# One-hot rows in steps of eight tokens, two coefficient blocks at a time, and one up product moved behind the last block

## The chip, the core and the metric

The kernel runs on one core of a Trainium2 chip. Its engines work side by side and meet through semaphores: TensorE multiplies matrices (PE in the profile; PEld is its weight load), VectorE (DVE), ScalarE (ACT) and GpSimd (POOL) do elementwise work, SyncE (SP) issues most DMA transfers. The metric is the device time of one execution in microseconds (us); lower is better.

## The reference

Two transformer blocks run over 256 tokens of width 1024. The first has two layers, each with a mixer and then a product-key mixture of experts ("peer"), which is where this change lies:

```python
q = (t @ w_q).reshape(n_tok, PEER_HEADS, 2, PEER_DKEY // 2)
sc = jnp.einsum('thpd,hpnd->thpn', q, sub_keys)
s1, i1 = lax.top_k(sc[:, :, 0], 16);  s2, i2 = lax.top_k(sc[:, :, 1], 16)
...                       # the best 16 of the 256 sums per head: eidx = i1 * 128 + i2
gate = jax.nn.softmax(top_s, axis=-1)
hid = jax.nn.gelu(jnp.einsum('td,thkd->thk', tc, u[ec]), approximate=False)
out = jnp.einsum('thk,thkd->td', gc * hid, v[ec])
```

There are 128 x 128 = 16384 experts, 8 heads and 16 choices per head, so 128 picks for each token. The second block (attention of two kinds and two feed-forward layers) isn't touched.

## The kernel before

The kernel computes the experts densely. It multiplies all tokens with all rows of `u` (the "up product": 128 chunks of 128 experts), takes the GELU, multiplies with a dense matrix of coefficients (the gate where a token picked that expert, zero elsewhere) and multiplies the result with `v` (the "down product"). Each f32 product is made of three: a weight tile in `ring` is split into `ring_hi` by ScalarE (`split_hi`, line 538) and `ring_lo` by VectorE (`split_lo`, line 544, which waits for `split_hi`), and TensorE multiplies `hi*hi`, `lo*hi` and `hi*lo` (lines 550 to 552). The ring has 4 slots of 512 KB; SyncE reloads a slot once `split_lo` has read it.

**The stage of the change** is segment `upcoef`, which runs once in each of the two layers. In it TensorE does 24 up products (8 steps of three matmuls each, so 192 steps, numbered q) and between them builds the coefficients, four tokens (one "block") at a time. The coefficients of a token are a product of one-hot matrices: `hot_second` (one row per pick, a one at the second key) as weights, and `hot_gated` (a one at the first key, times the gate, as a high and a low fp16 part) as the moving side. So a block is 4 x 2 = 8 matmuls of 128x128 in fp16 (line 910), after every third step; there are 64 blocks.

Who does what in the stage, for block c:

- VectorE (`one_hots`): `hot_first` (line 1999), `hot_second` (2000), then `hot_gated` from `hot_first` and the gates (2008, or 2004 where b = 0, for the low part alone). Before c % 8 = 2, 5 and 7 it does one `split_lo`.
- ScalarE (`gate_rows`, line 1376): the high part for the blocks with b = 0, in four instructions; it waits for `hot_first` of that block. It also copies each finished block out of PSUM in two instructions (`store_coef`, lines 1367 and 1368), takes the GELU of each finished up product (`gelu_beside`, 1352), does `split_hi`, and after every fourth block issues a DMA that spills half of the coefficients to DRAM (`spill`, 1382).
- TensorE (`coefficients`): waits for the PSUM bank (block c - 4 stored), `hots_ready` and, where b = 0, `act_gated`. The blocks of four are taken in the order 1, 0, 2, 3 (`ORDER`).

The order on each engine is written out by hand: for TensorE in the loop over q, for VectorE in the loop over c, for ScalarE in a loop over p, of which each turn ("pair") holds eight blocks and three up products. `split_hi` works two slots ahead of the up product in hand (`AHEAD` = 2): in turn p it makes slots 3p + 2, 3p + 3 and 3p + 4, while VectorE makes 3p + 1, 3p + 2 and 3p + 3. Behind the stage stand eight down products (line 896). The first of them needs `weigh(0)` on VectorE (lines 2029 to 2035), which needs the last block stored (`last_coef`) and, before the change, all 24 GELUs.

Of the kernel before, what the change touches and what calls it, by code (L numbers as in the profile page):

```python
# [24 lines left out]
P = 128  # L25
# [113 lines left out]
STEP_TOKENS = 4 * BLOCK  # L139
ORDER = [1, 0, 2, 3]  # L140
# [127 lines left out]
def build(nc, a):  # L268
    with ExitStack() as ctx:
# [20 lines left out]
        desk = sb("desk", [P, 3 * 2 * (P + 4 * HALF)])  # L290
        normed = desk[:, 0:K * TA].rearrange("p (k t) -> p k t", k=K)
        product = sb("product", [P, 2, S])
# [3 lines left out]
        rows = desk[:, :].bitcast(F16).rearrange("p (b n) -> p b n", b=3)  # L296
        last = product[:, :, :].rearrange("p b t -> p (b t)").bitcast(F16)
        hot_second = [x.rearrange("p (a e t) -> p a e t", a=2, t=2) for x in [rows[:, b, 0:P * BLOCK] for b in range(3)] + [rstd[:, 0:2 * P].bitcast(F16)]]
        hot_gated = [x.rearrange("p (x a e t) -> p x a e t", x=2, a=2, t=2) for x in [rows[:, b, P * BLOCK:3 * P * BLOCK] for b in range(3)] + [last]]
        hot_first = sb("hot_first", [P, 3, 2, NKEYS, 2], F16)  # L300
# [11 lines left out]
        gates16 = picks[:, 2:4, :].rearrange("p x s -> p (x s)").rearrange("p (k x t) -> p k x t", x=2, t=BLOCK)  # L312
# [83 lines left out]
        hidden = arena[:, 0:HELD * S].rearrange("p (h t) -> p h t", t=S)  # L396
        coef = arena[:, HELD * S:].rearrange("p (g t f) -> p g t f", t=S, f=BLOCK)
# [23 lines left out]
        val2raw = hot_first.rearrange("p b a e t -> p (b a e t)").bitcast(F32)[:, 0:2 * TA].rearrange("p (b t) -> p b t", b=2)  # L421
# [256 lines left out]
        def _(pe):  # L678
# [170 lines left out]
            def peer(l):  # L849
# [34 lines left out]
                def down(n, e, i=0, slots=4):  # L884
# [5 lines left out]
                    for t in range(NT):  # L890
                        by_hi, by_lo = [weighed[:, e % 4, x, t * P:(t + 1) * P] for x in range(2)]
# [8 lines left out]
                def coefficients(w, count):  # L900

                    b = count % 4

                    wait_bank(pe, w)
                    pe.wait_ge(hots_ready, count + 1)
                    if b == 0:
                        pe.wait_ge(act_gated, count // 4 + 1)
                    for t in range(BLOCK):
                        for x in range(2):
                            mm = pe.matmul(work[:, w % 4, t * P:(t + 1) * P], hot_second[b][:, t // 2, :, t % 2], hot_gated[b][:, x, t // 2, :, t % 2], start=(x == 0), stop=(x == 1))  # L910
                    mm.then_inc(bank_done[w % 4], 1)

                built = l * S // BLOCK
# [220 lines left out]
            def warm():  # L1134
                zeros = hot_first.rearrange("p b a e t -> p (b a e t)")
# [20 lines left out]
        def _(act):  # L1156
# [144 lines left out]
            def peer(l):  # L1301
# [48 lines left out]
                def gelu_beside(u):  # L1350
                    act.wait_ge(beside_done, l * BESIDE + u + 1)
                    act.activation(hidden[:, SEGMENTS[1][2] + u, :], acc[:, u % 4, 0:S], ACT.Gelu).then_inc(beside_free, 1)
# [17 lines left out]
                def gate_rows(j):  # L1370
                    act.wait_ge(gates_ready, l + 1)
                    act.wait_ge(hots_used, l * (S // BLOCK) + 4 * j + 1)
                    if j:
                        act.wait_ge(*done(W0[f"expert{l}.1"] + 4 * (j - 1) + ORDER.index(0)))
                    for t in range(BLOCK):
                        ins = act.activation(hot_gated[0][:, 0, t // 2, :, t % 2], hot_first[:, 0, t // 2, :, t % 2], ACT.Copy, scale=act_gates[:, j, t:t + 1])
# [8 lines left out]
                for x, (kind, e, h, steps) in enumerate(SEGMENTS):  # L1385
# [263 lines left out]
        def _(dve):  # L1649
# [318 lines left out]
            def peer(l):  # L1968
# [7 lines left out]
                by_block = lambda v: v.rearrange("p (k t) -> p k t", t=BLOCK)  # L1976
# [9 lines left out]
                def one_hots(count, tok, w):  # L1986

                    if w is not None:
                        dve.wait_ge(*done(w))
                    of = lambda x: picks[:, x, tok:tok + BLOCK]  # L1990
                    b, first = count % 4, hot_first[:, (0, 1, 2, 1)[count % 4], :, :, :]
                    if b == 0 and count:
                        dve.wait_ge(act_gated, count // 4)
                    if b and count > 4:
                        dve.wait_ge(hots_ready, count - 1)
# [429 lines left out]
```

## Time and profile before

| | us |
|---|---|
| median of 3 runs | 2471.43 (2470.43 to 2473.3) |
| the profiled execution | 2470.42 |
| its span in the trace | 2468.6 |
| TensorE busy | 2433.4 (99%) |
| VectorE busy | 1891.4 (77%) |
| ScalarE busy | 1256.3 (51%) |
| the stage of the change, each of two | about 106 |

The profile gives the busy time of each engine, the instructions by line with what ended the idle time before them, the waits by who waited for whom, and a timeline. "x8" in a timeline row means eight instructions merged; their start is that of the first. The mean of a short instruction is longer than the distance at which such instructions follow each other, since they are pipelined: the distance between two starts is what counts.

### The profile page before, as it was taken

To read this page: it belongs to the slowest core of one execution; us is meant where nothing else is said; L and a number is where in the kernel's file an instruction comes from. 1 tells how busy PE (TensorE), PEld (TensorE's weight loads), DVE (VectorE), ACT (ScalarE), POOL (GpSimd) and SP (SyncE) were. 2 spreads that over 40 slices of the span, in tenths; PEclk is the share of its full clock that TensorE was granted. 3 is DMA by queue.
4 is the path that set the end of the run, shared out by engine and by line. 5 is a ranking of instruction groups with operands and counts; after the bars stand their busy time and mean duration, and the time that the engine had idled before them with its cause. 6 is when DMAs were issued, how large, how long until landed. Compare 5 with 4: busy or idle time off the path is not lost.

```text
span 2468.6 us, 48181 instructions
## 1 busy us (share of the span) xinstructions
PE 2433.4 (99%) x17669; PEld 2253.8 (91%) x17669; DVE 1891.4 (77%) x3674; ACT 1256.3 (51%) x2092; POOL 132.4 (5%) x115
## 2 busy tenths in 40 slices
PE   9999999999999999999999999999999999999999
PEld 8999998999999888999988999999889999899999
DVE  6789997666666788889996666666887767887774
ACT  6755884444444434455874444444335445656343
POOL 0042000000000000052000000000000001100000
PEclk9999999999999999999999999999999999999999
DMA  7445677666665555546677666655554555634555
GB/s 241 143 158 184 191 204 249 207 214 213 210 200 188 188 187 171 189 146 201 188 219 236 213 210 207 213 196 188 187 187 144 174 183 182 142 103 156 182 182 165
DMA packets 191991, 465.16 MB, mean 188 GB/s; under 512 B 81530, under 2 KB 83706, under 8 KB 190944
## 3 DMA queue, kind: packets, MB, share of 16 engines
q1 hardware_dynamic: 118592, 419.47, 52.5%
q0 software_dynamic: 6624, 24.28, 3.3%
q10 hardware_dynamic: 66624, 19.40, 3.2%
q8 instruction: 94, 1.54, 0.3%
q14 instruction: 57, 0.47, 0.1%
HBM read 442.50 MB, written 20.59 MB: 188 GB/s over the span
## 4 chain that ended last, share of the span: by engine, by line
PE 49%; DVE 2%; ACT 1%; issue 0%; DMA 0%; DVEq 0%; ACTq 0%
PE acc L896 14%; PE work L550 9%; PE work L552 9%; PE work L551 9%; PE acc L550 2%; PE acc L551 1%; PE acc L552 1%; PE work L910 1%; PE work L1126 1%; DVE ring_lo L544 1%; PE work L1112 0%; PE work L1099 0%; DMA ring<-in_u 0%; ACT ring_hi L538 0%; PE work L1100 0%
## 5 line engine op out<-in xcount | busy, mean ns | idle before, releaser
L544 DVE TENSOR_TENSOR ring_lo<-ring,ring_hi 128x1024 fp32r<-128x1024 f32 (+1 forms) x757 | 918.8, 1217 | 421.0 <-ACT ring_hi L538 419.3
L538 ACT ACTIVATE ring_hi<-ring 128x1024 fp32r<-128x1024 f32 (+1 forms) x797 | 832.3, 1051 | 440.6 <-PE acc L896 359.8
L550 PE MATMUL work<-normed_hi,ring_hi 128*128 128x256 f32 (+1 forms) x2544 | 722.3, 284 | 10.2 <-DVE ring_lo L544 5.9
L551 PE MATMUL work<-normed_lo,ring_hi 128*128 128x256 f32 (+1 forms) x2544 | 713.3, 280 | 0.0
L552 PE MATMUL work<-normed_hi,ring_lo 128*128 128x256 f32 (+1 forms) x2544 | 713.3, 280 | 0.0
L896 PE MATMUL acc<-ring_hi,weighed 128*128 128x512 f32 x2048 | 587.3, 396 | 3.0 <-DVE weighed L2033 3.0
L550 PEld LDWEIGHTS work<-normed_hi,ring_hi 128*128 128x128 f32 x2544 | 478.7, 188 | 23.2 <-DVE ring_lo L544 7.1
L551 PEld LDWEIGHTS work<-normed_lo,ring_hi 128*128 128x128 f32 x2544 | 478.1, 188 | 8.3
L552 PEld LDWEIGHTS work<-normed_hi,ring_lo 128*128 128x128 f32 x2544 | 478.0, 188 | 0.0
L896 PEld LDWEIGHTS acc<-ring_hi,weighed 128*128 128x128 f32 x2048 | 372.2, 188 | 82.6 <-issue 3.2
L550 PE MATMUL work<-arena_parts,ring_hi 128*128 128x256 f32 (+1 forms) x1184 | 336.0, 284 | 2.8 <-DVE arena L2292 2.1
L552 PE MATMUL work<-arena_parts,ring_lo 128*128 128x256 f32 (+1 forms) x1184 | 332.4, 281 | 0.0
L551 PE MATMUL work<-arena_parts,ring_hi 128*128 128x256 f32 (+1 forms) x1184 | 332.4, 281 | 0.0
L896 PE MATMUL acc<-ring_lo,weighed 128*128 128x512 f32 x1024 | 321.4, 395 | 0.0
L1348 ACT ACTIVATE arena<-work 128x256 f32 (+1 forms) x192 | 73.8, 384 | 338.4 <-PE work L552 338.3
L896 PEld LDWEIGHTS acc<-ring_lo,weighed 128*128 128x128 f32 x1024 | 192.3, 188 | 46.4
L550 PEld LDWEIGHTS work<-arena_parts,ring_hi 128*128 128x128 f32 x1184 | 222.7, 188 | 4.6 <-DVE arena L2292 2.3
L551 PEld LDWEIGHTS work<-arena_parts,ring_hi 128*128 128x128 f32 x1184 | 222.8, 188 | 0.1
L552 PEld LDWEIGHTS work<-arena_parts,ring_lo 128*128 128x128 f32 x1184 | 222.6, 188 | 0.0
L2040 DVE TENSOR_TENSOR product<-arena 128x256 f32 (+1 forms) x254 | 157.0, 618 | 0.3 <-DVE weighed L2035 0.3
L550 PE MATMUL acc<-normed_hi,ring_hi 128*128 128x256 f32 x512 | 155.0, 303 | 0.0
L552 PE MATMUL acc<-normed_hi,ring_lo 128*128 128x256 f32 x512 | 143.2, 280 | 0.0
(304 smaller groups left out, 2411.2 us busy)
## 6 DMA issues: line engine op xcount, KB each, us to landing
ring<-in_u SPq DMA_DIRECT2D x256, 512.0 KB, 3.9
ring<-in_v SPq DMA_DIRECT2D x256, 512.0 KB, 4.2
ring<-in_ffn_in SPq DMA_DIRECT2D x88, 512.0 KB, 3.7
ring<-in_query SPq DMA_DIRECT2D x32, 512.0 KB, 3.8
ficients_of_later_chunks<-gate_b ACTq DMA_DIRECT2D x32, 512.0 KB, 4.9
arena<-ficients_of_later_chunks POOLq DMA_DIRECT2D x32, 512.0 KB, 4.0
ring<-in_ffn_out SPq DMA_DIRECT2D x32, 512.0 KB, 4.0
ring<-in_even_in SPq DMA_DIRECT2D x27, 512.0 KB, 4.5
```

Source lines behind the costliest of these rows:

```text
L538: act.activation(ring_hi[:, n % RING, 0:width], ring[:, n % RING, 0:width], ACT.Copy).then_inc(hi_ready, 1)
L544: eng.tensor_tensor(ring_lo[:, n % RING, 0:width], ring[:, n % RING, 0:width], ring_hi[:, n % RING, 0:width].bitcast(F32), ALU.subtract).t ...
L550: pe.matmul(out, w_hi, hi, start=start, stop=False, **more)
L551: pe.matmul(out, w_hi, lo, start=False, stop=False, **more)
L552: return pe.matmul(out, w_lo, hi, start=False, stop=stop, **more)
L896: mm = pe.matmul(acc[:, 2 * half + t, :], tokens, rows[:, m, half * 512:(half + 1) * 512], start=(e == 0 and x == 0), stop=(e == CHUNKS - ...
L910: mm = pe.matmul(work[:, w % 4, t * P:(t + 1) * P], hot_second[b][:, t // 2, :, t % 2], hot_gated[b][:, x, t // 2, :, t % 2], start=(x == ...
L1126: mm = pe.matmul(work[:, w % 4, t * P:S], v, prob2[:, u % 2, b, t:NT, :].rearrange("p t q -> p (t q)"), start=(b == 0), stop=(b == NT), sk ...
L1348: act.activation(into, work[:, w % 4, 0:S], ACT.Gelu).then_inc(bank_free[w % 4], 1)
L2040: dve.tensor_tensor(product[:, e % 2, :], hid, co, ALU.mult).then_inc(coef_read, 1)
```

## The change

A group of eight tokens (`GROUP`) takes the place of the block of four for VectorE and TensorE, so there are 32 groups of two blocks.

- VectorE builds the one-hot rows of a group with one instruction where it took one per block. For even groups it makes the low part and the high part of the last four tokens; ScalarE makes the high part of the first four. One `split_lo` stands before each group g with g % 4 = 1, 2 or 3.
- TensorE takes the two blocks of a group one behind the other. The groups are spread over the first 184 of the 192 steps, so that the 24th up product follows the last group.
- ScalarE's order in a turn p is written anew, with two forms (p below 4, and from 4 on). `gate_rows` for the next even group moves between two stores, and `split_hi(n + 1)` moves from ahead of `store(c + 3)` to behind it, its DMA included.
- The wait for all GELUs moves from VectorE's start of the down products to its second chunk, and TensorE gets waits of its own ahead of the first down product (for 23 GELUs, then 24).
- The rows lie in other places of SBUF (`desk`, and the last two rows of `hidden` in `arena`, so that the GELU of the 23rd up product waits for `hots_ready`).

```diff
+GROUP = 2 * BLOCK
+GROUPS = S // GROUP
+BEFORE_LAST = K * (24 - 1)
...
                     for t in range(NT):
+                        if e == 0:
+                            pe.wait_ge(beside_free, (l + 1) * BESIDE - 1 + t)
...
-                def coefficients(w, count):
+                def coefficients(w, c):
+                    g, b = c // 2, c // 2 % 2
                     wait_bank(pe, w)
-                    pe.wait_ge(hots_ready, count + 1)
-                    if b == 0:
-                        pe.wait_ge(act_gated, count // 4 + 1)
+                    pe.wait_ge(hots_ready, l * GROUPS + g + 1)
+                    if c % 4 == 0:
+                        pe.wait_ge(act_gated, (l * S // BLOCK + c) // 4 + 1)
...
-                            if q % 3 == 2:
-                                c = q // 3
-                                coefficients(w0 + c, built + c // 4 * 4 + ORDER[c % 4])
+                            for g in range(GROUPS):
+                                if q + 1 == -(-BEFORE_LAST * (g + 1) // GROUPS):
+                                    for c in (2 * g, 2 * g + 1):
+                                        coefficients(w0 + c, c // 4 * 4 + ORDER[c % 4])
...
                 def gate_rows(j):
                     act.wait_ge(gates_ready, l + 1)
-                    act.wait_ge(hots_used, l * (S // BLOCK) + 4 * j + 1)
+                    act.wait_ge(hots_used, l * GROUPS + 2 * j + 1)
                     if j:
-                        act.wait_ge(*done(W0[f"expert{l}.1"] + 4 * (j - 1) + ORDER.index(0)))
+                        act.wait_ge(*done(W0[f"expert{l}.1"] + 2 * (2 * j - 2) + 1))
...
-                            gate_rows(2 * p)
+                            if p == 0:
+                                gate_rows(0)
                             split_hi(act, n)
+                            late = p >= PAIRS // 2
                             store(c)
                             store(c + 1)
-                            gelu_beside(u)
+                            if not late:
+                                gelu_beside(u)
                             store(c + 2)
+                            gate_rows(2 * p + 1)
+                            store(c + 3)
                             split_hi(act, n + 1)
-                            store(c + 3)
-                            gate_rows(2 * p + 1)
+                            gelu_beside(u if late else u + 1)
                             store(c + 4)
-                            gelu_beside(u + 1)
                             store(c + 5)
                             split_hi(act, n + 2)
+                            gelu_beside(u + 1 if late else u + 2)
                             store(c + 6)
-                            gelu_beside(u + 2)
+                            if p < PAIRS - 1:
+                                gate_rows(2 * p + 2)
                             store(c + 7)
+                            if late:
+                                gelu_beside(u + 2)
...
+                def one_hots(g, w):
+                    count, b, tok, final = l * GROUPS + g, g % 2, g * GROUP, g == GROUPS - 1
+                    first = hot_first[0 if final else g % 2]
+                    if g % 2 == 0 and count or final:
+                        dve.wait_ge(act_gated, (count + 1) // 2)
+                    if count >= 2:
+                        dve.wait_ge(hots_ready, count if final else count - 1)
+                    shape = [P, 4, P, 2]
...
                     dve.tensor_tensor(first, keys, row(0), ALU.is_equal).then_inc(hots_used, 1)
+                    if g >= 2:
+                        dve.wait_ge(*done(w + 2 * (g - 2) + 1))
                     dve.tensor_tensor(hot_second[b], keys, row(1), ALU.is_equal)
...
-                        for c in range(S // BLOCK):
-                            j, b = c // 4, c % 4
-                            if c % 8 in (2, 5, 7):
-                                split_lo(dve, base + c // 8 * 3 + (2, 5, 7).index(c % 8) + 1)
-                            one_hots(built + c, BLOCK * c, w0 + 4 * (j - 1) + ORDER.index(b) if j else None)
+                        for g in range(GROUPS):
+                            if g % 4:
+                                split_lo(dve, base + g // 4 * 3 + g % 4)
+                            one_hots(g, w0)
```

Three places show how the instructions now stand. ScalarE first, in turn p = 1: from the GELU of the turn's first up product (L1352) on, before the change. L1367 and L1368 are a store, L538 is `split_hi`, L1376 `gate_rows`.

```order
L1352 ACTIVATE arena<-acc 128x256
L1367 ACTIVATE gate_b<-work 128x4x16x4
L1368 ACTIVATE arena<-work 128x4x16x4
L538 ACTIVATE ring_hi<-ring 128x1024
L1367 ACTIVATE gate_b<-work 128x4x16x4
L1368 ACTIVATE arena<-work 128x4x16x4
L1382 DMA coefficients_of_later_chunks<-gate_b 128x16x64
L1376 ACTIVATE desk<-hot_first,const 128x128 x4
```

The same stretch after the change, where L1361 is the GELU, L1376 and L1377 the store, L1385 `gate_rows`, L542 `split_hi`:

```order
L1361 ACTIVATE arena<-acc 128x256
L1376 ACTIVATE gate_b<-work 128x4x16x4
L1377 ACTIVATE arena<-work 128x4x16x4
L1385 ACTIVATE desk<-desk,const 128x128 x4
L1376 ACTIVATE gate_b<-work 128x4x16x4
L1377 ACTIVATE arena<-work 128x4x16x4
L1391 DMA coefficients_of_later_chunks<-gate_b 128x16x64
L542 ACTIVATE ring_hi<-ring 128x1024
L1361 ACTIVATE arena<-acc 128x256
```

`split_hi` stood behind one store; now it stands behind two stores, the four instructions of `gate_rows` and the issue of a DMA.

VectorE, before, from one `split_lo` (L544) to the next, with two blocks between them:

```order
L544 TENSOR_TENSOR ring_lo<-ring,ring_hi 128x1024
L1999 TENSOR_TENSOR hot_first<-keys,picks 128x512
L2000 TENSOR_TENSOR desk<-keys,picks 128x512
L2008 TENSOR_TENSOR desk<-hot_first,picks 128x1024
L1999 TENSOR_TENSOR hot_first<-keys,picks 128x512
L2000 TENSOR_TENSOR desk<-keys,picks 128x512
L2008 TENSOR_TENSOR desk<-hot_first,picks 128x1024
L544 TENSOR_TENSOR ring_lo<-ring,ring_hi 128x1024
```

After, from the `split_lo` (L548) of group 3 on: an odd group (L2013, L2016, L2025) and the next even one (L2020 and L2021 are its low part and the half of its high part):

```order
L548 TENSOR_TENSOR ring_lo<-ring,ring_hi 128x1024
L2013 TENSOR_TENSOR arena<-keys,picks 128x1024
L2016 TENSOR_TENSOR desk<-keys,picks 128x1024
L2025 TENSOR_TENSOR desk<-arena,picks 128x2048
L2013 TENSOR_TENSOR desk<-keys,picks 128x1024
L2016 TENSOR_TENSOR desk<-keys,picks 128x1024
L2020 TENSOR_TENSOR desk<-desk,picks 128x1024
L2021 TENSOR_TENSOR desk<-desk,picks 128x512
```

The work is the same, in fewer and longer instructions: 14 for eight blocks where there were 24, beside the three `split_lo`.

TensorE at the end of the stage, before:

```order
L550 MATMUL acc<-normed_hi,ring_hi 128x256
L551 MATMUL acc<-normed_lo,ring_hi 128x256
L552 MATMUL acc<-normed_hi,ring_lo 128x256
L910 MATMUL work<-product,rstd 128x128 x8
L896 MATMUL acc<-ring_hi,weighed 128x512 x2
```

and after, at the last group and then at the first down product, with 21 rows of up product left out between the two fences:

```order
L556 MATMUL acc<-normed_hi,ring_lo 128x256
L917 MATMUL work<-desk 128x128 x16
L554 MATMUL acc<-normed_hi,ring_hi 128x256
L555 MATMUL acc<-normed_lo,ring_hi 128x256
L556 MATMUL acc<-normed_hi,ring_lo 128x256
```

```order
L554 MATMUL acc<-normed_hi,ring_hi 128x256
L555 MATMUL acc<-normed_lo,ring_hi 128x256
L556 MATMUL acc<-normed_hi,ring_lo 128x256
L902 MATMUL acc<-ring_hi,weighed 128x512 x2
L902 MATMUL acc<-ring_lo,weighed 128x512 x2
```

24 matmuls now stand between the last coefficients and the first down product; there were none.

## Rows read from the trace of the kernel before

**Rows 1.** Busy time by window, both stages: PE, PEld, DVE, ACT, POOL, clock, DMA.

```profile
258.00:364.00 106.00, 104.34 (x1095) 99.52 (x1093) 105.41 (x217) 89.49 (x239) 0.00 (x0) 1.00 0.71 199
1172.00:1278.00 106.00, 104.28 (x1094) 99.41 (x1092) 105.28 (x216) 89.59 (x240) 0.00 (x0) 1.00 0.72 198
```

**Rows 2.** Waits in 1172 to 1278: us in total, times, longest.

```profile
PEld work L910 <- issue: 4.3, 16, 0.8
```

**Rows 3.** Timeline of PE around one block: start us, us, what.

```profile
1175.58 0.63 PE L910 MATMUL work<-desk 128*128 128x128 f16 x8
1176.02 0.37 PE L550 MATMUL acc<-normed_hi,ring_hi 128*128 128x256 f32 x1
1176.23 0.28 PE L551 MATMUL acc<-normed_lo,ring_hi 128*128 128x256 f32 x1
...
1177.05 0.28 PE L552 MATMUL acc<-normed_hi,ring_lo 128*128 128x256 f32 x1
```

**Rows 4.** Timeline of ACT, the store of that block.

```profile
1176.31 0.38 ACT L1367 ACTIVATE gate_b<-work 128x256 f32<-128x256 f32 x1 [0.65 <-PE work L910]
```

**Rows 5.** Timeline of ACT: a store, the spill's issue, gate rows, a store, a GELU.

```profile
1193.35 0.38 ACT L1368 ACTIVATE arena<-work 128x256 f32<-128x256 f32 x1
1193.76 0.37 ACTq L1382 DMA_DIRECT2D ficients_of_later_chunks<-gate_b  x1
1194.25 1.32 ACT L1376 ACTIVATE desk<-hot_first,const 128x128 f16<-128x128 f16 x4 [0.52 <-ACT arena L1368]
1195.44 0.36 ACT L1367 ACTIVATE gate_b<-work 128x256 f32<-128x256 f32 x1
...
1195.96 0.38 ACT L1352 ACTIVATE arena<-acc 128x256 f32<-128x256 f32 x1
```

**Rows 6.** Timeline of DVE: one split and one block's one-hot rows.

```profile
1204.58 1.22 DVE L544 TENSOR_TENSOR ring_lo<-ring,ring_hi 128x1024 fp32r<-128x1024 f32 x1
1205.72 0.42 DVE L1999 TENSOR_TENSOR hot_first<-keys,picks 128x512 f16<-128x512 f16 x1
...
1206.39 0.69 DVE L2008 TENSOR_TENSOR desk<-hot_first,picks 128x1024 f16<-128x1024 f16 x1
1206.99 0.42 DVE L1999 TENSOR_TENSOR hot_first<-keys,picks 128x512 f16<-128x512 f16 x1
```

**Rows 7.** Timeline of ACT, then DVE, where split_lo waits for split_hi.

```profile
1302.47 1.06 ACT L538 ACTIVATE ring_hi<-ring 128x1024 fp32r<-128x1024 f32 x1 [2.10 <-PE acc L896]
...
1303.56 1.22 DVE L544 TENSOR_TENSOR ring_lo<-ring,ring_hi 128x1024 fp32r<-128x1024 f32 x1 [0.66 <-ACT ring_hi L538]
```

**Rows 8.** Timeline around 1246: a block that waits for VectorE's rows.

```profile
1245.56 0.69 DVE L2008 TENSOR_TENSOR desk<-hot_first,picks 128x1024 f16<-128x1024 f16 x1
...
1246.40 0.39 PE L910 MATMUL work<-desk 128*128 128x128 f16 x4
```

**Rows 9.** Timeline at the end of the stage: last block, last store, first down product.

```profile
1277.25 0.63 PE L910 MATMUL work<-product,rstd 128*128 128x128 f16 x8
...
1277.92 0.38 ACT L1364 ACTIVATE arena<-work 128x256 f32<-128x256 f32 x1
...
1279.39 0.70 PE L896 MATMUL acc<-ring_hi,weighed 128*128 128x512 f32 x2 [1.51 <-DVE weighed L2033]
```

**Rows 10.** Timeline of PE: its longest late wait.

```profile
2236.71 0.28 PE L552 MATMUL work<-arena_parts,ring_lo 128*128 128x256 f32 x1
2239.04 0.38 PE L550 MATMUL work<-arena_parts,ring_hi 128*128 128x256 f32 x1 [2.06 <-DVE arena L2292]
```

**Rows 11.** The window around that wait, columns as in Rows 1.

```profile
2225.00:2245.00 20.00, 15.43 (x121) 14.44 (x120) 11.61 (x26) 11.93 (x22) 0.00 (x0) 1.00 0.27 84
```

**Rows 12.** Timeline at the stage's start: first one-hot rows, TensorE's first matmul.

```profile
1171.49 0.43 DVE L1999 TENSOR_TENSOR hot_first<-keys,picks 128x512 f16<-128x512 f16 x1
...
1172.43 0.28 PE L550 MATMUL acc<-normed_hi,ring_hi 128*128 128x256 f32 x1
```

**Rows 13.** DMA issues on the page: KB each, us to landing.

```profile
ring<-in_u SPq DMA_DIRECT2D x256, 512.0 KB, 3.9
```

More of the change, by code:

```diff
@@ L289, in build @@
         lead_gain = sb("lead_gain", [P, 2, K])
-        desk = sb("desk", [P, 3 * 2 * (P + 4 * HALF)])
+        desk = sb("desk", [P, 14 * 256])
         normed = desk[:, 0:K * TA].rearrange("p (k t) -> p k t", k=K)
-        product = sb("product", [P, 2, S])
+        product = desk[:, 9 * 256:11 * 256].rearrange("p (b t) -> p b t", b=2)
         sub_keys = desk[:, 0:16 * NKEYS].rearrange("p (h e) -> p h e", e=NKEYS)
[L296 to L300, printed above, removed]
+        hot_zeros = desk[:, 11 * 256:].bitcast(F16)
         with nc.sbuf_tensor("gate_b", [P, K, S], F32) as gate_b:
@@ L396, in build @@
         hidden = arena[:, 0:HELD * S].rearrange("p (h t) -> p h t", t=S)
+        pieces = desk[:, :].bitcast(F16).rearrange("p (n x) -> p n x", x=GROUP * NKEYS)
+        last_held = arena[:, (HELD - 2) * S:HELD * S].bitcast(F16)
+        hot_second = [pieces[:, n, :].rearrange("p (a e t) -> p a e t", e=NKEYS, t=2) for n in (0, 3)]
+        hot_gated = [pieces[:, n:n + 2, :].rearrange("p x (a e t) -> p x a e t", e=NKEYS, t=2) for n in (1, 4)]
+        hot_first = [v.rearrange("p (a e t) -> p a e t", e=NKEYS, t=2) for v in (pieces[:, 6, :], last_held)]
         coef = arena[:, HELD * S:].rearrange("p (g t f) -> p g t f", t=S, f=BLOCK)
@@ L898, in down @@
                     mm.then_inc(chunk_used, 1)
[L900 to L902 removed]
+                def coefficients(w, c):
+                    g, b = c // 2, c // 2 % 2
                     wait_bank(pe, w)
[L905 to L907 removed]
+                    pe.wait_ge(hots_ready, l * GROUPS + g + 1)
+                    if c % 4 == 0:
+                        pe.wait_ge(act_gated, (l * S // BLOCK + c) // 4 + 1)
                     for t in range(BLOCK):
                         for x in range(2):
[L910 removed]
+                            at = c % 2 * 2 + t // 2
+                            mm = pe.matmul(work[:, w % 4, t * P:(t + 1) * P], hot_second[b][:, at, :, t % 2], hot_gated[b][:, x, at, :, t % 2], start=(x == 0), stop=(x == 1))
                     mm.then_inc(bank_done[w % 4], 1)
[L913 removed]
                 pe.wait_ge(normed_ready, K * (l + 1))
@@ L1134, in warm @@
             def warm():
-                zeros = hot_first.rearrange("p b a e t -> p (b a e t)")
+                zeros = hot_zeros
                 pe.wait_ge(warm_ready, 1)
@@ L1984, in peer @@
                 c0 = l * CHUNKS
[L1986 to L1995, printed above, removed]
-                    shape = [P, 2, P, 2]
+                def one_hots(g, w):
[6 more added lines that the diff above has]
+                    shape = [P, 4, P, 2]
@@ L2000, in one_hots @@
                     dve.tensor_tensor(hot_second[b], keys, row(1), ALU.is_equal)
                     dve.wait_ge(hots_used, count + 1)
-                    if b == 0:
-                        gate = gates16[:, tok // BLOCK, 1, :].rearrange("p (a t) -> p a t", t=2)
-                        dve.tensor_tensor(hot_gated[b][:, 1, :, :, :], first, gate.unsqueeze(2).to_broadcast(shape), ALU.mult).then_inc(hots_ready, 1)
+                    if g % 2 == 0:
+                        high, low = [gates16[:, g, x, :].rearrange("p (a t) -> p a t", t=2).unsqueeze(2).to_broadcast(shape) for x in range(2)]
+                        dve.tensor_tensor(hot_gated[b][:, 1, :, :, :], first, low, ALU.mult)
+                        dve.tensor_tensor(hot_gated[b][:, 0, 2:4, :, :], first[:, 2:4, :, :], high[:, 2:4, :, :], ALU.mult).then_inc(hots_ready, 1)
@@ L2300, in branch @@
                 low_part(K - 1)
-            dve.memset(hot_first[:, :, :, :, :], 0.0).then_inc(warm_ready, 1)
+            dve.memset(hot_zeros, 0.0).then_inc(warm_ready, 1)
             first_parts()
```

20 lines of the change are left out of this document (11 added, 9 removed).

## The prediction

> **What bounds the kernel now.** I read the busy time by window first, at the two stages that the change touches. In both, VectorE is busy for 105.3 to 105.4 of 106 us, TensorE for 104.3, ScalarE for 89.5 [rows 1]: both of the first two are full, so the question is who waits for whom. In the waits of one stage TensorE loses 4.3 us in 16 waits [rows 2], two in every eight blocks, most of them like the one at 1246.40, where a block starts 0.15 after VectorE's last row instruction for it ends (1245.56 + 0.69 = 1246.25) [rows 8].
>
> So VectorE sets the pace. From the distances of its starts, an instruction of 512 fp16 elements takes 0.335 (two in 0.67), one of 1024 0.60, a split 1.14 [rows 6]. Eight blocks are 16 + 2 of the first, 6 of the second and 3 splits: 6.03 + 3.60 + 3.42 = 13.05 us. TensorE by itself: a step of three matmuls is 0.351 (seven starts in 0.82 us, 0.117 each), and a block costs 0.53 (1175.58 to 1176.23 less one 0.12) [rows 3], so eight blocks and 24 steps are 4.24 + 8.42 = 12.66. The difference, 0.39 for each eight blocks, is the waiting.
>
> TensorE's whole stage, from 1172.43 [rows 12] to the first down product at 1279.39 [rows 9], is 106.96. By the same terms: 192 x 0.351 = 67.4, 64 x 0.53 = 33.9, waits 4.3, and 1.6 at the end, where the last block must be stored and weighed (1279.39 - 1277.25 - 0.53). That is 107.2; the terms hold to 0.2.
>
> **VectorE's part gets shorter.** Doubling 512 elements adds 0.27, so 2048 elements should take 0.60 + 2 x 0.265 = 1.13, 1.22 to the end (nearest rows: 0.69 for 1024 [rows 6]; at the rate of the f32 split, 2.2). An even group is 3 x 0.60 + 0.335 = 2.14, an odd one 2 x 0.60 + 1.13 = 2.33. Four groups and three splits: 8.94 + 3.42 = 12.36 instead of 13.05, 5.5 us less in a stage, if VectorE never waits.
>
> **TensorE's part gets shorter.** The second block of a group adds between 0.44 (the start of the matmul behind the eight) and 0.53 (nothing saved) [rows 3]; I take 0.48, so a group is 1.01. Work of a stage: 67.4 + 32 x 1.01 = 99.7, against 101.3.
>
> **The end of the stage.** The wait of 1.6 goes. With the last block's start as B, its store starts at B + 0.79 (behind the store of the block before: done at B - 0.48 + 0.73 [rows 4], plus 0.54), and store start to down product is now 1.47 [rows 9]: B + 2.3. The 24th up product ends at B + 0.53 + 2.81 = B + 3.3, and hides all of it, with 1.0 to spare. The new waits of TensorE and of the second chunk for the 24th GELU are covered by the first half of the first down product. I cost them at nothing; if that cover failed, it would be about 1 us per stage.
>
> **ScalarE's new order, the heart of the prediction.** `split_hi(n + 1)` makes slot 3p + 3. VectorE wants it for the `split_lo` ahead of group 4p + 3, and everything of that group (`hot_first`, `hot_second`, `hot_gated`) is queued behind that `split_lo`. Before, it stood ahead of the store; now two stores, `gate_rows` and a DMA issue stand ahead of it, and they wait for group 4p + 1 of TensorE. Let G be the start of group 4p + 1 there. Then
> - block c + 2 is stored from G + 0.73 (1175.58 to 1176.31) [rows 3, 4]; a store takes 0.52 (1195.44 to 1195.96) [rows 5]: G + 1.25
> - `gate_rows`: 1.19 (1194.25 to 1195.44) [rows 5]: G + 2.44. Its input, the `hot_first` of group 4p + 2, is there by then
> - store of c + 3, to its second instruction: 0.26; from there through the DMA issue to the next instruction: 0.90 (1193.35 to 1194.25) [rows 5]: `split_hi` starts at G + 3.60. The DMA's issue can't cost less than to its own end, 1193.76 + 0.37, which would be 0.12 less
> - `split_hi` to `split_lo`: 1.09 (1302.47 to 1303.56) [rows 7]: G + 4.69; VectorE was free at about G + 3
> - `split_lo` 1.14, two rows of 0.60, 1.22 for 2048 elements and 0.15 to TensorE [rows 6, 8]: group 4p + 3 starts at G + 8.40
>
> TensorE's own work from G to there is 11 steps and two groups, 3.86 + 2.02 = 5.88. So it waits 2.5 us, once in every turn of ScalarE's loop. VectorE makes up for none of it: it can't pass its own waiting split. Eight turns: 20.2, and about 0.2 more where the first turn starts and the last group waits for ScalarE's last rows.
>
> A second wait lies in turns 0 to 3. There `gelu_beside(u + 2)` stands ahead of a store and of the `gate_rows` for group 4p + 4, and its up product ends x = 1, 2, 3, 4 steps behind group 4p + 3 (steps 24, 48, 72, 96 against 23, 46, 69, 92). From the start of group 4p + 3: 1.01 + 0.35x + 0.19 until the GELU may start (0.31 behind its last matmul's start, as for the block in [rows 3, 4]), 0.27, a store 0.52, `gate_rows` 1.32 + 0.15: 3.46 + 0.35x. TensorE wants the rows for the second block, at 1.01 + 6 x 0.351 + 0.48 = 3.60. It waits 0.35x - 0.14: 0.2, 0.6, 0.9 and 1.3, together 2.9. With 0.2 at group 30 (the GELU of the 21st up product) the waits are 23.5 us a stage, where they were 4.3.
>
> SyncE's loads follow the splits. A slot's load has about three splits' time, over 10 us, and lands in 3.9 [rows 13]; I cost it at nothing. GpSimd is idle in the stage, and its reload of coefficients starts later by what the stage loses.
>
> **The sum.** A stage becomes 99.7 + 23.5 = 123.2, against 107.2: +16.0, and there are two: +32. From the profiled execution (2470.42, span 2468.6) that gives 2502.4; the median lies 1 us above it, so 2503.4, and I say 2503. The rest of the kernel is paced by TensorE and moves as a block.
>
> **Rivals.**
> - *The faster machine* (the other side). Decided by when `split_hi` starts: VectorE gets to its `split_lo` at G + 3, so if ScalarE reached it by G + 1.9 instead of 3.6, the wait would be gone. Then VectorE paces: 1171.49 [rows 12] + 8 x 12.36 + 0.2 = 1270.6 for the last group, + 1.01 + 2.81 = 1274.4 for the first down product instead of 1279.39, -5.0 a stage, 2461. With the GELU waits kept, some 2466. For it speaks that both engines' work really falls; against it, that each term ahead of `split_hi` is a measured row and none can be passed in the queue. 5%.
> - *Half of the wait.* ScalarE gets ahead by 1.2 us in each turn: 16 x 1.2 = 19 less, 2484. 6%, and 2% more for a time within 0.2% of now.
> - *Long fp16 rows at the f32 rate.* If 1024 and 2048 elements ran at the split's rate (1.14 and 2.2), eight blocks would cost VectorE 2 x (3.42 + 0.34 + 2.28 + 2.2) + 3.42 = 19.9, and a stage 159: +55, 2580. Against it: line 2008 has 1024 fp16 elements in 0.60 [rows 6]. 3%.
> - *TensorE's clock.* The profile grants 1.00 in both stages [rows 1]. TensorE would now idle for 2.5 us in every 14.6. The nearest row is a wait of 2.33 (2236.71 to 2239.04) [rows 10], in whose window the granted clock stays 1.00, the level of 2.4 GHz [rows 11]; nothing in the trace shows the lower level. If it fell to 1.2 GHz for both stages, TensorE's 99.7 would be near 200 and most waits would vanish in it: 2650 and more. 4%. The Trainium skill ("TensorE: Matmul & The Clock Gate", section "HAM oscillation — how this bites in real kernels") says that waits between groups of matmuls can send the clock back to half; by that rule the time would be this rival's, by the row it stays.
>
> **How the numbers follow.** Forecast 80%. Its own range: the 2.5 us of each turn are a sum of eight rows, and 0.7 either way in each of 16 turns (0.12 for the DMA issue, 0.2 for the 2048 elements, the rest for latencies between engines) is 11 us; the second block's 0.44 to 0.53 is 3 us. That gives 2490 to 2518. The rivals below hold 13% (2461, 2466, 2484, no change) and those above 7%; 20% stay out, so 2490 to 2518 is also the range given. A measurement of this kernel can tell 0.2% (5 us) from no change: faster 5%, same 2%, slower 93%.
>
> **What would show it.** In the profile after: L548 (`split_lo`) idle before it, put down to L542 (`split_hi`), some 1.5 us in each of 16 turns; TensorE's L917 waiting 2.5 us at groups 3, 7, 11 and so on, and 0.2 to 1.3 at groups 4, 8, 12 and 16; VectorE's share of the stage down from 99% to about 80%; 2048 elements at 1.22; no wait ahead of L902; granted clock 1.00. If L548 waits for nobody, the forecast is wrong at its center.

## The result, and the profile after

The changed kernel takes 2516.6 us (median of 4 runs, 2514.39 to 2517.26), the kernel before in the same comparison 2472.1 (4 runs, 2470.43 to 2473.3). The ratio is 1.018 with an interval of 1.0161 to 1.0197: it is 44.5 us slower, where 32 were forecast and 2518 was the end of the range.

| | before | after |
|---|---|---|
| profiled execution | 2470.42 us | 2517.04 us |
| its span | 2468.6 | 2515.2 |
| stage of the first layer, TensorE's first matmul to first down product | 106.91 | 129.22 |
| the same of the second layer | 106.96 | 131.06 |
| waits of TensorE in it, from the distances of its starts | 4.1 | 22.9 and 23.2 |

The two stages grew by 22.3 and 24.1 us, together 46.4 of the 46.6 that the span grew: the rest of the kernel kept its length to 0.2. The busy time by window of after, for both stages (PE, PEld, DVE, ACT, POOL, the granted clock, DMA share, GB/s), answers to [rows 1]:

```profile
255.00:385.00 130.00, 109.26 (x1103) 106.20 (x1103) 104.17 (x144) 89.20 (x246) 0.00 (x0) 0.94 0.59 167
1190.00:1325.00 135.00, 113.79 (x1124) 110.73 (x1123) 106.96 (x151) 89.34 (x247) 0.00 (x0) 0.92 0.59 166
```

VectorE was busy for 99% of the stage and is now for 80 and 79%; TensorE fell from 98% to 84%. So neither of the two paces the stage any more. And one number stands here that the forecast didn't have: the granted clock is 0.94 and 0.92, where it was 1.00. The waits of the second stage (us in total, times, longest) answer to [rows 2]:

```profile
DVE ring_lo L548 <- ACT ring_hi L542: 26.2, 15, 3.1
PEld work L917 <- issue: 23.1, 11, 2.8
...
PE work L917 <- DVE desk L2025: 19.3, 8, 2.6
...
ACT ring_hi L542 <- ACT arena L1377: 5.5, 11, 0.5
...
PE work L917 <- ACT desk L1385: 1.9, 2, 1.1
```

VectorE's `split_lo` (L548) waits for ScalarE's `split_hi` (L542), 26 us of a stage. Before, the same wait came to this:

```profile
DVE ring_lo L544 <- ACT ring_hi L538: 0.3, 1, 0.3
```

TensorE's blocks (L917) wait for the last row instruction of VectorE (L2025) eight times. From start to start, less the 0.12 of a matmul, these waits are 2.48 to 2.8 us; the profile counts some 0.16 less, up to the modelled end of the matmul ahead. Waits of TensorE are given from start to start from here on. The chain in one turn, first on ScalarE:

```profile
1201.05 0.38 ACT L1376 ACTIVATE gate_b<-work 128x256 f32<-128x256 f32 x1 [1.55 <-PE work L917]
...
1201.66 1.32 ACT L1385 ACTIVATE desk<-desk,const 128x128 f16<-128x128 f16 x4
1202.85 0.36 ACT L1376 ACTIVATE gate_b<-work 128x256 f32<-128x256 f32 x1
...
1203.51 0.37 ACTq L1391 DMA_DIRECT2D ficients_of_later_chunks<-gate_b  x1
1203.98 1.06 ACT L542 ACTIVATE ring_hi<-ring 128x1024 fp32r<-128x1024 f32 x1 [0.50 <-ACT arena L1377]
```

then on VectorE, which has nothing to do from 1203.12 on, since its queue is in order:

```profile
1202.70 0.42 DVE L2021 TENSOR_TENSOR desk<-desk,picks 128x512 f16<-128x512 f16 x1
1205.07 1.23 DVE L548 TENSOR_TENSOR ring_lo<-ring,ring_hi 128x1024 fp32r<-128x1024 f32 x1 [1.95 <-ACT ring_hi L542]
1206.21 0.68 DVE L2013 TENSOR_TENSOR arena<-keys,picks 128x1024 f16<-128x1024 f16 x1
1206.82 0.68 DVE L2016 TENSOR_TENSOR desk<-keys,picks 128x1024 f16<-128x1024 f16 x1
1207.42 1.22 DVE L2025 TENSOR_TENSOR desk<-arena,picks 128x2048 f16<-128x2048 f16 x1
1208.55 0.68 DVE L2013 TENSOR_TENSOR desk<-keys,picks 128x1024 f16<-128x1024 f16 x1
```

and on TensorE, with what stands behind the wait:

```profile
1200.32 1.09 PE L917 MATMUL work<-desk 128*128 128x128 f16 x16
...
1203.41 1.09 PE L917 MATMUL work<-desk 128*128 128x128 f16 x16
...
1206.03 0.28 PE L556 MATMUL acc<-normed_hi,ring_lo 128*128 128x256 f32 x1
1208.78 1.62 PE L917 MATMUL work<-desk 128*128 128x128 f16 x16 [2.48 <-DVE desk L2025]
...
1210.73 0.41 PE L556 MATMUL acc<-normed_hi,ring_lo 128*128 128x256 f32 x1
1210.95 0.41 PE L554 MATMUL acc<-normed_hi,ring_hi 128*128 128x256 f32 x1
...
1212.60 0.28 PE L556 MATMUL acc<-normed_hi,ring_lo 128*128 128x256 f32 x1
1212.72 0.28 PE L554 MATMUL acc<-normed_hi,ring_hi 128*128 128x256 f32 x1
...
1213.42 1.09 PE L917 MATMUL work<-desk 128*128 128x128 f16 x16
```

The sum of the forecast can be laid beside this turn, with G = 1200.32: block c + 2 stored at G + 0.73 (forecast 0.73), `gate_rows` at G + 1.34 (1.25), the next store at G + 2.53 (2.44), `split_hi` at G + 3.66 (3.60), `split_lo` at G + 4.75 (4.69), group 4p + 3 at G + 8.46 (8.40).

Behind the wait the same group takes 1.62 instead of 1.09 and the matmuls start 0.21 apart instead of 0.12, up to 1212.4. From group to group are 3.09 us (1200.32 to 1203.41), here 4.64 (1208.78 to 1213.42): 1.55 more, for the same instructions. Five short windows of after, with the columns as above, say what that is:

```profile
1208.00:1209.00 1.00, 0.22 (x4) 0.25 (x5) 1.00 (x2) 0.00 (x0) 0.00 (x0) 1.00 0.87 340
1209.00:1210.00 1.00, 1.00 (x15) 1.00 (x12) 1.00 (x3) 0.00 (x0) 0.00 (x0) 0.55 0.30 119
1210.00:1211.00 1.00, 1.00 (x8) 1.00 (x7) 1.00 (x3) 0.00 (x0) 0.00 (x0) 0.50 0.00 0
...
1212.00:1213.00 1.00, 1.00 (x9) 1.00 (x8) 1.00 (x2) 1.00 (x5) 0.00 (x0) 0.74 0.06 16
1213.00:1214.00 1.00, 1.00 (x15) 0.96 (x15) 1.00 (x2) 0.82 (x4) 0.00 (x0) 1.00 0.86 188
```

The granted clock falls within 1209 to 1210, just behind the start of the group, to 0.50, the level of 1.2 GHz, with 8 matmuls in a microsecond instead of 15; within 1212 to 1213 it rises again. This stands behind 11 of the 16 waits (turns 0, 2, 3, 5 and 7 of the first layer, 0, 1, 3, 4, 5 and 7 of the second). Measured from group to group against the same pieces of e1_split_early (below), with the waits taken off, TensorE loses 1.4 to 1.6 us to each, 16.5 in all.

At the end of the stage, VectorE's first and last instructions on `weighed` for the first down product, and the product, answer to [rows 9]:

```profile
1323.11 0.23 DVE L2052 CAST weighed<-desk 128x128 fp32r<-128x128 f32 x1
...
1324.26 0.29 DVE L2054 TENSOR_TENSOR weighed<-desk,weighed 128x128 fp32r<-128x128 f32 x1
...
1326.20 0.62 PE L902 MATMUL acc<-ring_hi,weighed 128*128 128x512 f32 x2
```

The first of the product's operands is there 2.9 us before TensorE starts it, the last 1.7 before. The wait of 1.51 ahead of the first down product is gone, as forecast. The forecast gave 1.0 to spare; 1.5 of the 2.9 is a slow stretch behind the last group, which makes TensorE late here.

### The profile page after: what moved, and what is told of

It is laid out like the page before. It is cut to its first block, busy times and chain, and to the rows that moved or that the text cites. A ratio compares the mean times of both kernels' runs of the same rounds, so it can differ in the third digit from the quotient of the medians.

```text
span 2515.2 us, 47938 instructions
## 1 busy us (share of the span) xinstructions
PE 2445.8 (97%) x17669; PEld 2269.6 (90%) x17669; DVE 1883.7 (75%) x3514; ACT 1250.1 (50%) x2092; POOL 132.3 (5%) x115
## 4 chain that ended last, share of the span: by engine, by line
PE 47%; DVE 2%; ACT 2%; issue 1%; ACTq 0%; DVEq 0%
PE acc L902 14%; PE work L554 9%; PE work L556 9%; PE work L555 9%; PE acc L554 1%; PE acc L556 1%; PE acc L555 1%; DVE ring_lo L548 1%; PE work L1133 1%; PE work L917 1%; ACT ring_hi L542 1%; ACT desk L1385 0%; DVE desk L2025 0%; PE work L1119 0%; PE work L1106 0%
## 5 line engine op out<-in xcount | busy, mean ns | idle before, releaser
L548 DVE TENSOR_TENSOR ring_lo<-ring,ring_hi 128x1024 fp32r<-128x1024 f32 (+1 forms) x757 | 919.3, 1218 | 471.2 <-ACT ring_hi L542 469.3
L542 ACT ACTIVATE ring_hi<-ring 128x1024 fp32r<-128x1024 f32 (+1 forms) x797 | 832.7, 1052 | 451.0 <-PE acc L902 360.4
L554 PEld LDWEIGHTS work<-normed_hi,ring_hi 128*128 128x128 f32 x2544 | 478.7, 188 | 22.3 <-DVE ring_lo L548 7.3
L2059 DVE TENSOR_TENSOR desk<-arena 128x256 f32 (+1 forms) x254 | 157.6, 620 | 4.5 <-ACT arena L1361 4.5
L555 PE MATMUL acc<-normed_lo,ring_hi 128*128 128x256 f32 x512 | 149.9, 293 | 0.0
```

The source lines that it names most:

```text
L542: act.activation(ring_hi[:, n % RING, 0:width], ring[:, n % RING, 0:width], ACT.Copy).then_inc(hi_ready, 1)
L548: eng.tensor_tensor(ring_lo[:, n % RING, 0:width], ring[:, n % RING, 0:width], ring_hi[:, n % RING, 0:width].bitcast(F32), ALU.subtract).t ...
L554: pe.matmul(out, w_hi, hi, start=start, stop=False, **more)
L555: pe.matmul(out, w_hi, lo, start=False, stop=False, **more)
L2059: dve.tensor_tensor(product[:, e % 2, :], hid, co, ALU.mult).then_inc(coef_read, 1)
```

## The experiments

Two things were to be told apart. First, whether the order on ScalarE is the cause of the waits. **Theory:** `split_hi(n + 1)` behind the stores makes all of them, and this one line moved ahead of them makes the grouped kernel at least as fast as the one before. **Rival:** the groups themselves, longer row instructions and buffers that come free later, are what costs. Second, what the forecast's missing 12 us are. **Theory:** TensorE's clock. **Rival:** waits larger than in the sum.

| kernel | time us (runs) | ratio to before, 95% interval | stages us | clock |
|---|---|---|---|---|
| after | 2516.6 (4) | 1.0179, 1.0161 to 1.0197 | 129.2, 131.1 | 0.993 |
| e1_split_early | 2469.7 (10) | 0.9994, 0.9984 to 1.0004 | 106.6, 106.2 | 1.000 |
| e2_gelu_late | 2463.3 (6) | 0.9969, 0.9957 to 0.9982 | 102.6, 102.6 | 1.000 |
| e3_filled_wait | 2500.6 (4) | 1.0119, 1.0102 to 1.0136 | 122.4, 122.0 | 0.999 |
| e4_gelu_late_alone | 2509.0 (4) | 1.0149, 1.0132 to 1.0166 | 125.8, 127.0 | 0.994 |
| e5_no_up_behind | 2460.8 (5) | 0.9958, 0.9945 to 0.9972 | 101.6, 101.4 | 0.999 |
| e6_before_split_late | 2491.9 (4) | 1.0085, 1.0069 to 1.0100 | 116.4, 116.4 | 0.999 |
| e7_two_steps_behind | 2459.6 (5) | 0.9953, 0.9940 to 0.9967 | 100.8, 100.9 | 0.999 |
| e8_filled_in_part | 2500.6 (4) | 1.0121, 1.0106 to 1.0137 | 122.4, 122.0 | 1.000 |

The kernel before ran beside them at 2471.4 (e1 to e4) and 2471.3 (e5 to e8). The clock is the mean of the profiled execution.

**e1_split_early**: the changed kernel with one line moved. `split_hi(n + 1)` stands ahead of `store(c + 2)`, one store earlier than even in the kernel before.

```diff
+                            split_hi(act, n + 1)
                             store(c + 2)
                             gate_rows(2 * p + 1)
                             store(c + 3)
-                            split_hi(act, n + 1)
                             gelu_beside(u if late else u + 1)
```

> One line of the changed kernel is moved: in ScalarE's loop split_hi(n + 1) stands ahead of store(c + 2) instead of behind store(c + 3), so that neither the two stores nor gate_rows nor the DMA issue stand between it and the time when VectorE wants it. Theory (the late split is the cause, the clock its follower): VectorE's wait for ScalarE's split goes, TensorE's 16 waits of 2.5 us shrink to 0.3 to 0.6 each, the granted clock is 1.00 again in both stages, and a stage falls from 129 to 131 us to about 106.5. Waits: 23 to 7 us a stage, and 6 to 8 us of slow clock gone: 2516.6 - 2 x 23 = about 2470 (2465 to 2475). Rival (the grouping itself holds TensorE: longer VectorE instructions, two banks at a time): the waits stay and the time is 2505 or more.

Measured: 2469.7, 47 us less than after and no different from before by more than 0.2%. Its waits from 1175 to 1300 (the second stage ends at 1278.5):

```profile
PEld work L917 <- issue: 7.4, 13, 1.3
...
DVE ring_lo L548 <- ACT ring_hi L542: 5.4, 7, 1.3
```

and both stages by window:

```profile
250.00:360.00 110.00, 105.22 (x1119) 102.12 (x1118) 105.25 (x149) 89.50 (x244) 0.00 (x0) 1.00 0.69 197
1170.00:1278.00 108.00, 102.74 (x1106) 99.70 (x1105) 102.29 (x143) 87.49 (x243) 0.00 (x0) 1.00 0.71 200
```

All 16 waits of 2.5 us are gone, and with them every stretch at the lower clock. What is left are 4.4 us ahead of groups and the waits of the second block for `gate_rows` behind a GELU, 0.25, 0.6, 0.95 and 1.3 in turns 0 to 3, 7.7 and 7.4 us in all where 4.1 were before. That eats most of what the shorter work (2.4, see the ledger below) and the end of the stage (1.6) gave. Moving this one line takes away the whole loss; the groups of eight alone cost nothing of it. The place behind `store(c + 2)`, which the line had before, was not run with groups; by the sum of the forecast `split_hi` would start there at G + 1.25, early enough (an estimate).

**e6_before_split_late**: the other way round, the late `split_hi` alone in the kernel before, without any grouping. It stands behind three stores and `gate_rows` here, one store later than in the changed kernel, so the two places are alike and not the same.

```diff
                             store(c + 2)
-                            split_hi(act, n + 1)
                             store(c + 3)
                             gate_rows(2 * p + 1)
                             store(c + 4)
+                            split_hi(act, n + 1)
                             gelu_beside(u + 1)
```

> The kernel before, with one line moved the other way: split_hi(n + 1) stands behind store(c + 3), gate_rows and store(c + 4) instead of ahead of store(c + 3), much as the change puts it. Theory (the place of the split alone costs the time, whatever the size of the groups): VectorE starts its third split of a turn late, waits 0.7 to 1 us of which it can make up nothing, since it sets the pace; TensorE waits 1.8 us per turn in three pieces under 0.9 each instead of 0.4 in two; no long idle time, so the granted clock stays 1.00. +9.6 us a stage: 2471.4 + 19 = 2490 (2483 to 2496). Rival (the late split hurts only in groups of eight tokens): under 2475.

Measured: 2491.9, 20.6 slower than before, both stages 9.4 to 9.5 longer; 1.6 us of its longer span lie outside the two and are not explained. Its waits from 1175 to 1300, the second stage and little more:

```profile
PEld work L910 <- issue: 14.0, 24, 0.8
...
DVE ring_lo L544 <- ACT ring_hi L538: 10.1, 9, 1.2
```

So the order costs without the groups too, but less. In every turn there are three waits, 0.77, 0.26 and 0.71 (1.74) instead of one of 2.5. As I read it, a block of four tokens needs less of VectorE behind the split than a group of eight (0.335 + 0.335 + 0.69 against 0.60 + 0.60 + 1.22), and TensorE asks for it in smaller pieces. None is long, and the clock stays up.

**e3_filled_wait**: the changed kernel, with 20 more matmuls ahead of the wait at every fourth group. They write a bank that the group's own first matmuls overwrite.

```diff
                     wait_bank(pe, w)
+                    if c % 8 == 6:
+                        for _ in range(20):
+                            pe.matmul(work[:, w % 4, 0:S], text_hi[:, 0, 0:P], text_hi[:, 0, :], start=True, stop=True)
                     pe.wait_ge(hots_ready, l * GROUPS + g + 1)
```

> The changed kernel with 20 more matmuls of the up product's kind (256 columns, 2.34 us at 0.117 each) written into the free PSUM bank of group 4p + 3 just ahead of the wait for its rows; the group's own first matmul overwrites them. TensorE is late by 2.5 us there anyway, so they lie in the wait. Theory (the clock falls because TensorE idles in that wait): granted clock 1.00 in both stages, waits of some 0.2 us left at these places, time 2516.6 - 14 = 2503 (2499 to 2507), which is the forecast without the clock. Rival (the clock falls for another reason, or only the records show it): 2516 or, as more power is drawn, above.

Measured: 2500.6, 16.0 less than after with more work in it. Its second stage by window, and its waits from 1175 to 1300:

```profile
1180.00:1310.00 130.00, 127.35 (x1318) 124.64 (x1317) 109.37 (x156) 92.21 (x251) 0.00 (x0) 1.00 0.62 177
```

```profile
DVE ring_lo L548 <- ACT ring_hi L542: 17.3, 13, 2.0
```

VectorE still waits for `split_hi` as the sum of the forecast has it, TensorE gets to its groups no sooner, but the clock is 1.00. This is the kernel that the forecast described: 122.4 and 122.0 a stage (forecast 123.2), with 0.25, 0.6, 0.95 and 1.3 inside groups as in e1, 2500.6 (forecast 2503). The other 16 us are the clock's; the pieces above gave 16.5.

**e8_filled_in_part**: the same with 8 matmuls instead of 20.

```diff
-                        for _ in range(20):
+                        for _ in range(8):
```

> The changed kernel with 8 filler matmuls instead of 20 in the wait of group 4p + 3: 0.94 us of work, so TensorE still idles for 1.6 us there. The wait itself is as long, only the clock can differ. If any idle time of some length sends the clock down in part of the turns, the granted clock is between 0.993 and 1.00 and the time between 2501 and 2516; if an idle time of 1.6 us is short enough, it is 1.00 and the time 2501 (2499 to 2503), as with 20. I expect the latter at 60%.

Measured: 2500.6, the same as e3. In its second stage TensorE idles again, 1.45 to 1.75 us at a time (PE 116.55 of 130, in e3 127.35), and yet:

```profile
1180.00:1310.00 130.00, 116.55 (x1221) 113.16 (x1220) 109.24 (x156) 92.16 (x251) 0.00 (x0) 1.00 0.62 176
```

```profile
PE work L920 <- DVE desk L2028: 9.4, 7, 1.4
```

Its stages have the length of e3's to 0.1 us. Idle time of 1.45 to 1.75 us in each turn leaves the clock alone; 2.48 to 2.8 brought it down in 11 of 16.

**e2_gelu_late**: e1, and the GELUs late in all turns.

```diff
-                            late = p >= PAIRS // 2
+                            late = True
```

> As the run before, and the GELUs of all eight turns stand where the changed kernel has them from the fifth turn on (the last one behind store(c + 7)), so that no GELU stands ahead of gate_rows for the next even group. Theory: the second kind of wait (0.2, 0.6, 0.9, 1.3 us in turns 0 to 3) goes, some 3 us a stage, and 0.2 of the first kind in each of these turns: 2470 - 8 = 2462 (2459 to 2466), under the kernel before. Rival (the GELU order costs nothing, the waits inside a group are of another kind): same as the run before.

Measured: 2463.3, 6.4 less than e1 and 0.3% faster than before. The waits of its second stage (1170 to 1273):

```profile
PEld work L917 <- issue: 4.0, 9, 0.8
PE work L917 <- DVE desk L2025: 2.4, 8, 0.6
```

No wait stands inside a group any more; each turn keeps one of 0.39. That is the old picture with smaller numbers: VectorE paces with 12.36 a turn, TensorE follows.

**e4_gelu_late_alone**: the same line in the changed kernel, the split left late.

> The changed kernel with the GELU order of its fifth turn in all turns, and split_hi(n + 1) left where it is. Theory: only the waits inside the groups 4, 8, 12 and 16 go, of which the trace shows 1.7 us in the first stage and 2.3 in the second: 2516.6 - 4 = 2512.6 (2508 to 2517, since the slow clock may come or go at a turn or two, 1.5 us each). Rival (the GELU order, not the split, makes most of the loss): under 2500.

Measured: 2509.0, 7.6 less than after. The window of its second stage:

```profile
1185.00:1320.00 135.00, 115.75 (x1152) 112.89 (x1151) 108.53 (x156) 92.28 (x251) 0.00 (x0) 0.94 0.61 172
```

The waits inside groups are gone, those of 2.5 us are not, and neither is the lower clock: it stands behind 9 of the 16 (turns 0, 2, 4 and 6 of the first layer, 0, 1, 3, 5 and 7 of the second) instead of 11. The waits fell by 4.6 us, near the 4 expected, and two slow stretches less gave 2.9 more; which turns have one differs from kernel to kernel.

**e5_no_up_behind**: e1 with all 24 up products spread between the groups, none behind the last, and GELUs early.

```diff
-BEFORE_LAST = K * (24 - 1)
+BEFORE_LAST = K * 24
...
-                            late = p >= PAIRS // 2
+                            late = False
```

> The kernel with split_hi moved early, in which the groups are spread over all 192 steps again (nothing stands behind the last group) and the GELUs keep the early places in every turn. It undoes the moving of the 24th up product. With six steps between any two groups TensorE's work per four groups is 12.46 us, VectorE's 12.36: TensorE sets the pace and waits only 0.2 us in the stage, and every group 4p + 4 has one step more of cover, so the GELU waits go too. The wait at the end comes back: store of two blocks and the first weighing, 1.7 to 2.1 us. By these terms a stage is 99.7 + 0.2 + 2 = 101.9 (the run with late GELUs: 102.6), so 2462 (2459 to 2465). Rival (the product behind the last group is worth its 1.6 us net): 2463.3 + 3 = 2466 or more.

Measured: 2460.8, 2.5 less than e2, though the wait ahead of the first down product is back:

```profile
1268.35 0.70 PE L902 MATMUL acc<-ring_hi,weighed 128*128 128x512 f32 x2 [1.74 <-DVE weighed L2052]
```

With 24 products between the groups TensorE needs 24 x 0.351 + 4 x 0.98 = 12.34 us a turn, with 23 only 8.07 + 3.92 = 11.99; VectorE needs 12.36. So the 24th product, taken out from between the groups, makes TensorE arrive 0.37 too early in every turn, 3 us a stage (e2 shows 0.39 a turn), to hide a wait of 2 at the end. The early GELUs cost nothing here, no wait inside a group is left in e5. The forecast's own rule for that wait, 0.35x - 0.14, would say so: with 24 products a group stands behind every sixth step, the third product of a turn ends right ahead of group 4p + 3 (24, 48, 72 steps), and x is 0.

**e7_two_steps_behind**: between the two; e2 with two steps of the 24th product behind the last group.

```diff
-BEFORE_LAST = K * (24 - 1)
+BEFORE_LAST = K * 24 - 2
```

> The kernel with split_hi early and all GELUs late, with the groups spread over 190 of the 192 steps: two steps (0.7 us) stand behind the last group instead of eight. Six steps between nearly all groups give VectorE the time it needs (waits 0.4 us a stage instead of 3), and of the 2 us at the end 0.7 are covered. A stage is 99.7 + 0.4 + 1.1 = 101.2: 2463.3 - 3.5 = 2460 (2457 to 2463), the fastest of the series. Rival (the end of the stage costs more than its terms once it isn't covered): 2463 or more.

Measured: 2459.6, the fastest of all, 0.47% below before (0.33 to 0.60). In a window of its second stage both engines are full, and the wait at the end is half as long as in e5. It is put down to a GELU here, since these stand late, and no longer to `weighed`:

```profile
1161.00:1263.00 102.00, 101.69 (x1101) 100.03 (x1100) 101.41 (x144) 86.93 (x240) 0.00 (x0) 1.00 0.72 207
```

```profile
1267.98 0.70 PE L902 MATMUL acc<-ring_hi,weighed 128*128 128x512 f32 x2 [0.88 <-ACT arena L1361]
```

e5 and e7 differ by 1.2 us, less than 0.1%; their stages (101.6 and 101.4 against 100.8 and 100.9) say the same as the times, but the times alone don't tell the two apart.

## Why the prediction was right, and where it was off

**Right in the mechanism, lucky at the edge.** The waits came out as summed. That the time lies inside the range, 1.4 us from its end, is luck: the width was given to the terms of the chain and to the second block, which came in close, and was used up by the clock, which had no place in the sum.

**The heart of it held.** The forecast read one line of ScalarE's new order, followed it through two stores, `gate_rows` and a DMA issue to VectorE and back to TensorE, and got 2.5 us a turn. All 16 turns have it, 2.48 to 2.8, and each of the six marks in the turn shown above lies within 0.1 of its sum. The idle time ahead of L548 was given as some 1.5 us; it is 1.95 there, since VectorE had been free since before G + 3. Waits of a stage were forecast at 23.5 and are 22.9 and 23.2. e1 shows that the place of this line is the cause, and e6 that a late split costs time without the groups too.

**The smaller terms.** 2048 elements take 1.22, 1024 0.68 and their starts lie 0.60 apart, as estimated. A group costs 0.98 (3.09 less six steps of 0.351), not 1.01, so that TensorE's work of a stage is 98.8 and not 99.7; without its waits e2 has 98.7 in both. This is most of what lies between e3's 122.4 and the 123.2 of the sum. The second wait, that of `gate_rows` behind the GELU, was given as 0.2, 0.6, 0.9, 1.3. e1 has 0.25, 0.6, 0.95 and 1.3. In the changed kernel only some of them show (0.6, 0.3, 0.6 and 0.95, 1.3): where TensorE is at the lower clock it comes late itself and waits less. The end of the stage cost nothing, as forecast. In the rival of long fp16 rows, 159 is VectorE's work alone, 52 over the stage of 107; its +55 holds only with the last group and the last product added.

**The term that was mis-sized: the clock.** The prediction made TensorE's clock a rival of its own, all or nothing: either 1.00 throughout, by the wait of 2.33 at 2236.71 [rows 10, 11], or down for both stages, 2650 and more. It was neither. The clock fell behind single waits and came back within the same turn, 16.5 us by the trace and 16.0 by e3 (2516.6 less 2500.6). The two mistakes are plain now. The nearest row was one wait of 2.33 (2.21 when counted as these are), shorter than the 2.5 that were forecast and a single case; it does not bound 16 longer ones. And a lower clock needn't last: its price is to be worked out for each wait. Between two groups TensorE has 3.09 us of work; had the lower level held for one such piece behind each wait, that would have been at most 3.1 us a turn, so the term's bounds were 0 and 49 us. 11 turns at 1.5 came out. With that term the range would have reached beyond 2518, which the time came close to.

The Trainium skill ("TensorE: Matmul & The Clock Gate", section "HAM oscillation — how this bites in real kernels") has this picture, from a kernel whose waits are for loads and longer than these: every wait sends the clock to half anew, and the loss is half of the time that is then spent throttled. The trace agrees in kind: the level is down from about 1209.1 to 1212.5, and the 1.55 lost there is somewhat under half of that. It differs in that 5 of the 16 waits had no such stretch behind them, and the prediction was wrong to read the section as a time of 2650.

**The ledger.** Per trace, for both stages together: waits 46.1 instead of 8.3, +37.8; the lower clock +16.5; the wait at the end -3.2; TensorE's own work, 98.8 instead of 101.2 a stage, -4.8. That is +46.3 of the 46.4 measured. The forecast had +38.4, 0, -3.2 and -3.2.

**What stays open.** Why five of the 16 waits, of the same length as the others, left the clock at 1.00. It isn't the length (2.51 stands on both sides), and it isn't the turn: in e4, with the same waits, turn 4 of the first layer has a slow stretch and turn 3 has none, in after it is the other way round. No run has idle times between 1.75 and 2.48 at these places.

## What to carry to other kernels

When an instruction is moved back on an in-order engine, write down what each instruction now ahead of it waits for: here one line put a helper for the next engine behind work of the last one, and closed a circle of three engines that had been open (TensorE's group, ScalarE's stores and split, VectorE's rows for the next group); the line moved ahead took away the whole loss of 1.8%, and with the GELUs and the last product placed anew the kernel was 0.3 to 0.5% faster than before. Price the clock per wait and not per kernel where a busy TensorE gets regular waits like these 2.5 us, and compare a wait with rows on either side of its length. And of two engines that are nearly level, don't take work from between the one's pieces to hide a wait at the end before the pace of the other has been multiplied by the number of turns (e2 against e5 and e7).

## What the runs showed of the hardware

- TensorE's clock fell to 0.50 behind 11 of 16 waits of 2.48 to 2.8 us in a stream that was otherwise full, and rose again in the same turn, while TensorE worked (in the one shown, it is down from about 1209.1 to 1212.5). Each cost 1.4 to 1.6 us. With 1.45 to 1.75 us of idle time at the same places (e8), and with waits of under 0.8 in every turn (e6), it stayed at 1.00.
- Matmuls that do nothing but fill a wait made a kernel faster: 2516.6 to 2500.6, and 8 of them did as much as 20.
- fp16 `tensor_tensor` of 512, 1024 and 2048 elements: starts 0.335, 0.60 and 1.13 us apart, 0.42, 0.68 and 1.22 to their own end.
